# Up products of a mixture-of-experts item of 129 to 192 tokens with the weights stationary

## The reference, cut to what matters

```
scores = sigmoid(h @ router_w);  8 of 64 experts per token (4 of 8 groups), weights normalised x 2.5
per expert e, on its tokens xb (n x 1024):
  hid = silu(xb @ w1[e]) * (xb @ w3[e])     # w1, w3: 1024 x 256
  y[tokens] += (hid @ w2[e]) * weight       # w2: 256 x 1024
y + shared expert, times a gate, added to the residual stream
```

## Time and profile before

| | us |
|---|---|
| median of 3 runs | 2477.16 (2475.75 to 2477.36) |
| profiled execution | 2461.14 |
| its span | 2459.4 |
| PE busy | 2400.4 (98%) |
| DVE busy | 1179.6 (48%) |
| POOL busy | 616.1 (25%) |
| ACT busy | 482.6 (20%) |

### The profile page before, as it was taken

How to read it: one execution, slowest core, us unless ns; L and a number is a source line. 1 busy time by engine, 2 the same in 40 slices (tenths; PEclk the granted TensorE clock), 3 DMA queues, 4 the chain that set the end, 5 groups by cost and what they waited for, 6 DMA issues and landing times.

```text
span 2459.4 us, 32897 instructions
## 1 busy us (share of the span) xinstructions
PE 2400.4 (98%) x8544; PEld 1175.8 (48%) x8545; DVE 1179.6 (48%) x2744; ACT 482.6 (20%) x892; POOL 616.1 (25%) x628
## 2 busy tenths in 40 slices
PE   6999999999999999999999999999999999999997
PEld 3444444555544556665444455444444444444443
DVE  3377212666755666657335676443333333343332
ACT  3311000444432133333211112200000000000000
POOL 0000000000022100000211143555555545455441
PEclk9999999999999999999999999999999999999998
DMA  8132333443362333212433412599899999999995
GB/s 260 42 73 48 81 77 115 110 136 108 119 181 65 82 81 95 90 44 86 133 110 113 128 61 105 196 306 300 287 303 332 333 325 340 314 359 364 327 317 132
DMA packets 121190, 435.26 MB, mean 177 GB/s; under 512 B 21004, under 2 KB 23260, under 8 KB 95376
## 3 DMA queue, kind: packets, MB, share of 16 engines
q1 hardware_dynamic: 78208, 306.91, 35.8%
q0 software_dynamic: 42896, 127.25, 19.5%
HBM read 366.44 MB, written 71.70 MB: 178 GB/s over the span
## 4 chain that ended last, share of the span: by engine, by line
PE 89%; DVE 6%; DMA 1%; issue 1%; SPq 1%; ACT 1%; POOL 0%; DVEq 0%; POOLq 0%; ACTq 0%
PE psum L980 22%; PE psum L1462 17%; PE psum L1529 9%; PE psum L1065 8%; PE psum L1311 7%; PE psum L1467 5%; PE psum L1328 3%; PE psum L1268 2%; PE psum L1535 2%; PE psum L1372 2%; PE psum L1136 2%; PE psum L1146 2%; PE psum L1155 2%; PE psum L1395 1%; DMA mem<-in_ada_w 1%
## 5 line engine op out<-in xcount | busy, mean ns | idle before, releaser
L980 PE MATMUL psum<-mem 128*128 128x512 f32 x1536 | 690.2, 595 | 1.0 <-ACT mem L1656 1.0
L1462 PE MATMUL psum<-mem 128*128 x1008 | 449.9, 594 | 1.5 <-DVE mem L2673 1.0
L980 PEld LDWEIGHTS psum<-mem 128*128 128x128 f32 x1536 | 279.9, 191 | 294.4 <-issue 291.4
L785 POOL DMA_INDIRECT mem<-h_d,idx x287 | 293.7, 1023 | 354.6 <-DVE idx L2774 257.0
L1462 PEld LDWEIGHTS psum<-mem 128*128 128x128 f32 x1008 | 186.6, 190 | 229.6 <-issue 229.6
L2752 DVE TENSOR_TENSOR mem<-mem,psum 128x256 f32<-128x256 f32 x93 | 39.1, 421 | 419.0 <-ACT mem L1941 417.4
L1529 PE MATMUL psum<-mem 128*128 128x512 f32 x504 | 228.0, 599 | 1.0 <-issue 0.6
L1065 PE MATMUL psum<-mem 128*128 128x512 f32 x448 | 192.8, 592 | 0.0
L790 POOL DMA_INDIRECT out_x<-mem,put x93 | 140.5, 1510 | 99.0 <-issue 73.3
L1311 PE MATMUL psum<-mem 128*128 128x512 f32 x384 | 165.0, 592 | 0.0
L1529 PEld LDWEIGHTS psum<-mem 128*128 128x128 f32 x504 | 93.0, 190 | 124.6 <-issue 124.6
(11 more groups left out here) (421 smaller groups left out, 2488.4 us busy)
## 6 DMA issues: line engine op xcount, KB each, us to landing
mem<-in_exp_w SPq DMA_DIRECT2D x201, 1024.0 KB, 8.8
mem<-in_w_in SPq DMA_DIRECT2D x16, 2048.0 KB, 14.2
proj_d<-mem SPq DMA_DIRECT2D x104, 256.0 KB, 2.0
mem<-in_ada_w POOLq DMA_DIRECT2D x16, 1024.0 KB, 6.3
mem<-proj_d POOLq DMA_DIRECT2D x56, 256.0 KB, 3.0
mem<-proj_d POOLq DMA_DIRECT2D x20, 512.0 KB, 5.7
mem<-in_ada_w SPq DMA_DIRECT2D x4, 2048.0 KB, 23.0
mem<-in_w_branch SPq DMA_DIRECT2D x3, 2048.0 KB, 8.0
```

The source lines that it names most:

```text
L785: g.indirect_dma_start(x[:, 2 * P * n:2 * P * (n + 1)], None, h2_q, bass.IndirectOffsetOnAxis(ap=idx[:, p, j, n:n + 1], axis=0), bounds_ch ...
L980: mm = t.matmul(bank(unit_bank(u)), l, r, start=(k == 0), stop=(k == KD - 1))
L1462: return t.matmul(bank(up_banks[j][r]), xgT[r][:, k, P * j:P * (j + 1)], up_piece(h, r, k), start=(k == 0), stop=(k == KD - 1))
```

## The change: 192 tokens streamed past stationary weights

For an item of 129 to 192 tokens (size class 3: n in steps of 64, rounded up) the up products change sides. The weights are stationary, 128 columns of the hidden layer at a time (each second column, f = 0 and f = 1), and the 192 tokens are streamed. The result has hidden columns on partitions, w1's in the first 256 columns of a bank and w3's in the other 256, one bank for each f. silu and the product work on 256 columns as before, and the product is written straight into hidT: no transpose, no copy. The downs of such an item stay a full and a half tile. Items of other sizes keep their products. The semaphores e_hT and e_hc become one each, counted by turned tiles. The code for the last item behind PE's loop becomes one more turn of the loop.

```diff
+            MIDDLE = P + HALF
+            def up_middle(b, f, z, k):
+                w = w13[b][:, z, k, :].rearrange("p (n f) -> p f n", f=FK)[:, f, :]
+                return t.matmul(psum[:, up_banks[f][b % 2], FF * z:FF * z + MIDDLE], w, xgT[b % 2][:, k, 0:MIDDLE],
+                                start=(k == 0), stop=(k == KD - 1))
+            def up_middle_begin(b):
                 for k in range(KD):
-                    mm = up_half(1, b, k)
+                    up_middle(b, 0, 0, k)
+                for k in range(KD - 1):
+                    up_middle(b, 0, 1, k)
+            def up_middle_end(b):
+                up_middle(b, 0, 1, KD - 1).then_inc(e_H[0], 1)
+                for z in range(2):
+                    for k in range(KD):
+                        mm = up_middle(b, 1, z, k)
                 mm.then_inc(e_H[1], 1)
+            def by_buffer(part, h, r):
+                with pe.If(h > 0):
+                    part(2 + r)
+                with pe.Else():
+                    part(r)
+                pe.nop()
             def up_begin(n, h, r):
-                with pe.If(n > HALF):
-                    for k in range(UP_AHEAD):
-                        up(0, h, r, k)
+                with pe.If(pe.snap(sizes) == 3):
+                    by_buffer(up_middle_begin, h, r)
                 with pe.Else():
+                    with pe.If(n > HALF):
+                        for k in range(UP_AHEAD):
+                            up(0, h, r, k)
                     with pe.Else():
-                        up_half_begin(r)
+                        by_buffer(up_half_begin, h, r)
...
             def up_end(n, h, r):
+                with pe.If(pe.snap(sizes) == 3):
+                    seconds.up()
+                    by_buffer(up_middle_end, h, r)
                 with pe.Else():
+                    with pe.If(n > HALF):
...
+                        with pe.If(n > P):
+                            seconds.up()
+                            for k in range(KD):
+                                mm = up(1, h, r, k)
+                            mm.then_inc(e_H[1], 1)
...
             def down_second(n, p):
                 outs.wait(e_ob[1])
                 outs.up()
-                outs.wait(e_hc[1])
-                with pe.If(n > P + HALF):
+                with pe.If(n > MIDDLE):
+                    turned.wait(e_hc)
...
             def turn_hidden(n, now):
-                with pe.If(n > HALF):
-                    with pe.If(n > P):
+                with pe.If(n > P):
+                    with pe.If(n > MIDDLE):
                         seconds.wait(e_hid[1])
+                        turned.up()
+                        turned.up()
                         turn_tile(0)
+                        turn_tile(1)
+                    with pe.Else():
+                        seconds.wait(e_hid[1])
+                    pe.nop()
...
+                pe.reg_mov(sizes, pe.snap((n + HALF - 1) // HALF))
...
-            with pe.Fori(0, NI // 4) as it:
+            with pe.Fori(0, NI // 4 + 1) as it:
...
-            with pe.If(pe.snap(n_last) > 0):
-                turn_hidden(pe.snap(n_last), NI + 1)
-                downs(pe.snap(n_last), 1, 16 * (NI // 2), NI + 1)
...
             def hidden_rows(n, now, p):
+                    with dve.If(n > P + HALF):
...
+                    with dve.Else():
+                        dve.wait_ge(e_si[0], now)
+                        hidden(hidT[p][:, 0, :], 0, p)
+                        wide.wait(e_si[1])
+                        hidden(hidT[p][:, 1, :], 1, p)
```

More of the change, by code:

```diff
@@ L342, in layer_kernel @@
         e_xg = [two("xg0"), two("xg1")]
-        e_H, e_si, e_hid, e_hT, e_hc, e_O, e_ob = (two(n) for n in ("H", "si", "hid", "hT", "hc", "O", "ob"))
+        e_H, e_si, e_hid, e_O, e_ob = (two(n) for n in ("H", "si", "hid", "O", "ob"))
+        e_hT, e_hc = sem("e_hT"), sem("e_hc")
         e_w += [sem(f"e_w{b}") for b in (2, 3)]
@@ L346, in layer_kernel @@
         e_T, e_red, e_idx, e_lists, e_sc, e_up = (sem("e_" + n) for n in ("T", "red", "idx", "lists", "sc", "up"))
-        to_clear = [*e_xg[0], *e_xg[1], *e_H, *e_si, *e_hid, *e_hT, *e_hc, *e_O, *e_ob,
+        to_clear = [*e_xg[0], *e_xg[1], *e_H, *e_si, *e_hid, e_hT, e_hc, *e_O, *e_ob,
                     e_T, e_red, e_idx, e_lists, e_sc, e_up, *e_w[2:], *e_v[2:]]
@@ L1553, in downs @@
                 pe.wait_ge(e_ob[0], now)
-                pe.wait_ge(e_hc[0], now)
                 with pe.If(n > HALF):
@@ L1615, in pe_item @@
                     up_end(n, h, r)
-                    with pe.If(n > P):
-                        up_second(n, h, r)
-                    pe.nop()
                     pe.reg_mov(n_now, tokens(pe, i + 1))
@@ L1943, in hidden_turned @@
             def hidden_turned(j, p, n):
-                s.activation(hidT[p][:, :, P * j:P * j + n], psum[:, 1, FF * j:FF * j + 2 * n].rearrange("p (f n) -> p f n", f=FK), ACT.Copy).then_inc(e_hc[j], 1)
+                s.activation(hidT[p][:, :, P * j:P * j + n], psum[:, 1, FF * j:FF * j + 2 * n].rearrange("p (f n) -> p f n", f=FK), ACT.Copy).then_inc(e_hc, 1)
             act.wait_ge(s_ya, NT - 1)
             act.wait_ge(s_tab, 1)
-            for x in (*e_si, *e_hc):
+            for x in (*e_si, e_hc):
                 act.sem_inc(x, 1)
-            wide = Count(act, "wide")
+            wide, turned = Count(act, "wide"), Count(act, "turned")
             def act_item(it, q):
@@ L2749, in _, with hidden @@
             up_banks = ((4, 0), (5, 5))
-            def hidden(j, p):
-                v.tensor_tensor(hid[j], sg[:, j, :], bank(up_banks[j][p])[:, FF:2 * FF], ALU.mult).then_inc(e_hid[j], 1)
+            def hidden(dst, j, p):
+                v.tensor_tensor(dst, sg[:, j, :], bank(up_banks[j][p])[:, FF:2 * FF], ALU.mult).then_inc(e_hid[j], 1)
             def hidden_rows(n, now, p):
-                dve.wait_ge(e_si[0], now)
-                hidden(0, p)
                 with dve.If(n > P):
                     wide.up()
-                    wide.wait(e_si[1])
-                    hidden(1, p)
+                    with dve.If(n > P + HALF):
+                        dve.wait_ge(e_si[0], now)
+                        hidden(hid[0], 0, p)
+                        wide.wait(e_si[1])
+                        hidden(hid[1], 1, p)
+                    with dve.Else():
+                        dve.wait_ge(e_si[0], now)
+                        hidden(hidT[p][:, 0, :], 0, p)
+                        wide.wait(e_si[1])
+                        hidden(hidT[p][:, 1, :], 1, p)
+                    dve.nop()
+                with dve.Else():
+                    dve.wait_ge(e_si[0], now)
+                    hidden(hid[0], 0, p)
                 dve.nop()
```

94 lines of the change are left out of this document (37 added, 57 removed).

## The result

| | median us | all | runs | ratio to before (95%) |
|---|---|---|---|---|
| before | 2478.10 | 2471.86 to 2481.86 | 20 | |
| after | 2482.82 | 2476.43 to 2488.98 | 20 | 1.0023 [1.0016, 1.0030] |

The forecast was 2471.2, 6 us faster, with a range of 2464 to 2480. The change lost 4.7 us. Repeated later on another chip, where before took 2472.74, the same pair gave no difference: 1.0002 [0.9990, 1.0015]. The profiled execution of after took 2482.01 us (span 2480.3).

The account below looks back on a forecast made before the run. The prediction took PE's instruction stream to bound the expert stage, with the DMAs nearly full too. Up products -2.9, transposes -4.8 and control +1.7 gave -6.0 us, from 2477.16 to 2471.2, range 2464 to 2480.

Parts of the forecast that it names:

- Term 1: Up products of the 13 changed items: 64 instructions spaced 0.1635 us, 10.51 us an item for 10.73, gain 2.9 us.
- Rival A: Changed items' up products: the strided weight load sets the pace, +16 to +44 us (2493 to 2521); chance 0.13.
- Term 2: Transposes of the changed items' hidden result leave PE: 9 x 0.33 + 4 x 0.45, gain 4.8 us.
- Term 3: PE's added control flow: exposed only in the 17 small entries, 0.1 us each, 1.7 us lost; hidden elsewhere.
- Its small entries: The 17 small entries: control is exposed there, -0.1 to 0.3 us an entry, taken as 0.1, 1.7 us lost.
- so it runs ahead and hides the two branches within them: Changed items: the sequencer issues a pair in at most 0.112 us, the engine needs 0.16, so branches cost nothing.
- The fallback, 13 x 0.4 = 5.2: Changed items: if their two branches were uncovered, at 0.2 us each, they would cost 5.2 us.
- rival B: Whole kernel: no measurable change, products save nothing or branches in changed items are uncovered, 2474 to 2477 us; chance 0.33.
- Sum: Whole kernel: -2.9 - 4.8 + 1.7 = -6.0 us of work taken off PE, 2471.2 at the median.

Follow-up runs that it names:

- y_load: After, with PE's register read of the next item's token count moved ahead of up_begin: 2468.91 us, ratio 0.9975 to before.
- a_before: The kernel before, unchanged, run again for a second profile: 2478.49 us, ratio 1.0001 to before.
- x_dead: Before, with after's size class, branches and middle blocks added, which no item enters: 2486.35 us, ratio 1.0035 to before.
- b_epi: After, with before's epilogue restored behind the loop: 2482.97 us, ratio 1.0025 to before.
- y_best2: After, with four items written out and the early read of the token count, run a second time: 2462.50 us, ratio 0.9955 to before.
- z_best: Before, with four items written out and the early read of the token count: 2469.75 us, ratio 0.9990 to before.
- a_after: The kernel after, unchanged, run again for a second profile on another chip: 2473.51 us, ratio 1.0002 to before.
- y_order: After, with the blocks of the middle items placed behind the others: 2482.53 us, ratio 1.0023 to before.

## Why the prediction was wrong, point by point

**Term 1, right.** Spacing (5.04 - 0.329)/29 = 0.1625 us against 0.1635, and 10.50 us per clean item against 10.51. **Rival A fell:** a strided weight load takes 198 ns where the contiguous takes 190, and is hidden.

**Term 2, right in the work.** No transposes split the larger item's products any more: from 1681.51 L1463 runs x32 in 14.00 us without a break. Ahead of the four small entries part of the gain went to the late sequencer: the 32 instructions of L1468 at 2219.59 are followed by L1551 at 2224.09, 4.50 us with 0.58 of issue idle in it, where before took 4.86 with 0.32 (2199.66 to 2204.52).

**Term 3, the step that failed.** Its small entries were right, even too dear, where no other wait covers them: 1700.94 to 1705.54 is 4.60 us against 4.59 in the earlier trace rows. Wrong was the other half, "so it runs ahead and hides the two branches within them". That priced two branches against the rate of issue, and left out what stands behind up_end, above all the register read, whose move gave y_load 4.6 us; and it took the lead over a 192-column stream to be as good as over the 512-column one it replaced. After 2170 us the sequencer's delays show, where the prediction had nothing: 8.7 us for 1.0 in a_before. The fallback, 13 x 0.4 = 5.2, was of the right size and stood in the text only as a remark, with no chance of its own beyond rival B.

**A cost with no term: code.** Each block stands four times in the program (two places, two buffers). The prediction counted executed instructions only. x_dead shows what code that is never executed costs, 7.9 us, most of it in the first pass; its loop is 550 instructions longer than before's, after's 280. After has 5.0 us more of early idle than a_before and 1.3 of lower clock behind it.

**Sum.** -6.0 was forecast for the work. -5.4 remains in b_epi against a_before, once idle time is taken out; the same reckoning for y_best2 against z_best gives -6.0 - 5.3 + 3.2 = -8.1 (stage length, issue idle, waits on ScalarE and VectorE), where the medians differ by -7.2. So the size of the work was right to about 2 us. With 12.8 us more issue idle (15.4 against 2.6) after lost 4.7 where before was at 2478, and on chip D, with 9.6, nothing. The sign of the total turned on a term that wasn't in it. The base was also an untypical execution: it had 2.5 us of waits on ScalarE and VectorE where a_before has 14.4; this didn't enter the difference.

**Left open.** What holds the sequencer up in the middle of straight code, with no packet on its queue (at 1615 us and after 2170, most often in the same items), no run settles. The DMA engines were as full around clean items (0.96 to 1.04 of their share, over 11 us each in after and a_after, before 2400 us) as around the others (1.01 to 1.04). Nor is it settled how much of the gain from writing out is branches and how much the slower first pass, or why the loss is 0.2% in the first comparison and on chips A and B (b_epi, y_order), and nothing on D.

## What to carry to other kernels

Price a new branch by the code it adds and by what is queued on the engine while it is taken, not by the instructions that it executes: replacing long matmuls by many short ones spends the lead that had hidden register reads and branches. Look at the page's instruction queue: more packets than the program has blocks means that a loop is refetched. And hold a change against a base with the same loop form; here the change was worth -7 us in one form, and +5 (on one chip 0) in another. And look at the granted clock behind a gap: it can cost as much again as the gap.

## What the runs showed of the hardware

Code of 64 matmuls that is never executed moved a kernel from 2486 to 2951 us, by making its loop refetched (51 to 337 packets) and, with PE idle so often, by a granted clock of 0.82 to 0.89 in its stage. After a gap of 3.99 us the clock was 0.50 for 3 us (x_dead, 1599 to 1602), and ten instructions took 7.52 us in place of 4.55. A load of every second f32 as stationary operand takes 198 ns and hides behind a 192-column stream at 0.1625 us. PE's issue gaps grow as the stream narrows, 0.9, 2.5 to 4.9, and 10.6 us over the same 832 instructions at 256, 192 and 128 columns.
